# Later ones products for the norms, and one product with the values for both directions of a gated linear attention

## The reference

```
y = xf * lax.rsqrt(jnp.mean(xf * xf, axis=-1, keepdims=True) + EPS)
h = h + 0.5 * swiglu(rmsnorm(h, norm_gains[l, 0]), ...)
h = h + mixer(rmsnorm(h, norm_gains[l, 1]), ...)
h = h + 0.5 * swiglu(rmsnorm(h, norm_gains[l, 2]), ...)
```

```
att = jnp.where(mask, jnp.einsum('bhnid,bhnjd->bhnij', q_dec, k_inv), 0.0)
o_intra = jnp.einsum('bhnij,bhnjv->bhniv', att, vc)
...
o = (o_f + o_b)[:, :, pad:, :]
```

## Time and profile before

| | |
|---|---|
| median of 3 runs | 1885.31 us (1884.41 to 1885.64) |
| the profiled execution | 1884.92 us, of which the profile's span is 1883.6 us |
| granted TensorE clock, mean | 0.999 of full speed (2.4 GHz) |
| TensorE matmul busy | 1855.7 us, 99% of the span, 15211 instructions |
| VectorE busy | 1366.7 us, 73% |
| ScalarE busy | 1040.6 us, 55% |
| DMA | 365.92 MB, 194 GB/s in the mean |
| chain that ended last | TensorE 96%, ScalarE 2%, VectorE 1% |

### The profile page before, as it was taken

How to read it: one execution, slowest core, us unless ns; L and a number is a source line. 1 busy time by engine, 2 the same in 40 slices (tenths; PEclk the granted TensorE clock), 3 DMA queues, 4 the chain that set the end, 5 groups by cost and what they waited for, 6 DMA issues and landing times.

```text
span 1883.6 us, 36365 instructions
## 1 busy us (share of the span) xinstructions
PE 1855.7 (99%) x15211; PEld 1817.0 (96%) x15211; DVE 1366.7 (73%) x2353; ACT 1040.6 (55%) x1732; POOL 1.3 (0%) x8
## 2 busy tenths in 40 slices
PE   7999999999999999999999999999999999999998
PEld 7999998899999999999889999999999999999998
DVE  6777776576776678677658787698787558787744
ACT  6444564655444444456566455576565457656543
POOL 0000000000000000000000000000000000000000
PEclk9999999999999999999999999999999999999999
DMA  7776333356775577633235778454555554445553
GB/s 284 261 269 263 121 132 99 105 178 241 265 289 200 202 259 277 232 135 134 91 134 211 259 287 298 141 173 155 174 185 179 188 180 160 168 167 185 187 189 112
DMA packets 51811, 365.92 MB, mean 194 GB/s; under 512 B 6620, under 2 KB 8060, under 8 KB 9920
## 3 DMA queue, kind: packets, MB, share of 16 engines
q1 hardware_dynamic: 51648, 363.59, 55.2%
HBM read 362.52 MB, written 1.05 MB: 193 GB/s over the span
## 4 chain that ended last, share of the span: by engine, by line
PE 96%; ACT 2%; DVE 1%; issue 0%; DMA 0%; SPq 0%; DVEq 0%; ACTq 0%
PE bank L439 29%; PE bank L440 28%; PE bank L441 28%; PE bank L475 2%; PE bank L471 2%; PE bank L472 2%; PE bank L705 1%; PE bank L633 1%; PE bank L690 1%; PE bank L735 0%; PE bank L639 0%; PE bank L865 0%; PE bank L521 0%; ACT w_hi L1015 0%; PE bank L880 0%
## 5 line engine op out<-in xcount | busy, mean ns | idle before, releaser
L439 PE MATMUL bank<-xn_hi,w_hi 128*128 128x272 f32 (+3 forms) x2688 | 777.1, 289 | 1.7 <-DVE w_lo L1519 1.7
L441 PE MATMUL bank<-xn_lo,w_hi 128*128 128x272 f32 (+3 forms) x2688 | 764.3, 284 | 0.0
L440 PE MATMUL bank<-xn_hi,w_lo 128*128 128x272 f32 (+3 forms) x2688 | 764.2, 284 | 0.0
L439 PEld LDWEIGHTS bank<-xn_hi,w_hi 128*128 128x128 f32 (+1 forms) x2688 | 506.2, 188 | 9.4 <-issue 4.4
L440 PEld LDWEIGHTS bank<-xn_hi,w_lo 128*128 128x128 f32 (+1 forms) x2688 | 506.1, 188 | 1.2
L441 PEld LDWEIGHTS bank<-xn_lo,w_hi 128*128 128x128 f32 (+1 forms) x2688 | 506.8, 189 | 0.0
L1015 ACT ACTIVATE w_hi<-raw_a 128x1024 fp32r<-128x1024 f32 (+1 forms) x282 | 307.6, 1091 | 300.7 <-PE bank L441 263.9
L1015 ACT ACTIVATE w_hi<-raw_b 128x1024 fp32r<-128x1024 f32 (+1 forms) x282 | 307.5, 1091 | 282.3 <-PE bank L441 260.5
L1519 DVE TENSOR_TENSOR w_lo<-raw_a,w_hi 128x1024 fp32r<-128x1024 f32 (+1 forms) x282 | 356.5, 1265 | 135.5 <-ACT w_hi L1015 135.1
L1519 DVE TENSOR_TENSOR w_lo<-raw_b,w_hi 128x1024 fp32r<-128x1024 f32 (+1 forms) x282 | 356.6, 1265 | 133.0 <-ACT w_hi L1015 132.3
L439 PE MATMUL bank<-h_hi,w_hi 128*128 128x272 f32 (+1 forms) x704 | 201.7, 286 | 0.0
(11 more groups left out here) (316 smaller groups left out, 2624.2 us busy)
## 6 DMA issues: line engine op xcount, KB each, us to landing
raw_a<-in_weights SPq DMA_DIRECT2D x123, 1024.0 KB, 4.8
raw_b<-in_weights SPq DMA_DIRECT2D x123, 1024.0 KB, 4.8
ada_raw<-in_ada_w SPq DMA_DIRECT2D x48, 1024.0 KB, 5.0
raw_a<-in_weights SPq DMA_DIRECT2D x16, 1408.0 KB, 5.8
raw_b<-in_weights SPq DMA_DIRECT2D x16, 1408.0 KB, 5.9
c_rows<-in_c_rows SPq DMA_DIRECT2D x3, 512.0 KB, 5.8
raw_a<-in_weights SPq DMA_DIRECT2D x2, 768.0 KB, 4.1
raw_b<-in_weights SPq DMA_DIRECT2D x2, 768.0 KB, 4.2
```

The source lines that it names most:

```text
L439: pe.matmul(o, wh, xh, start=start, stop=False)
L440: pe.matmul(o, wl, xh, start=False, stop=False)
L441: return pe.matmul(o, wh, xl, start=False, stop=stop)
```

## The change

Two places are changed. First, `norm_sum` stands later within the leading steps: behind kk = 5 in the feed-forward stages of the first network (before: 1), behind kk = 3 in the first `ln1` stage (before: 2), behind kk = 2 in the mixers (before: 1). The stages `ff` and the second `ln1` keep kk = 2, and the very first stage keeps its place. Second, VectorE adds the two directions' masked scores of each head, and TensorE multiplies the sum with the values once instead of multiplying both. The sums lie in the first half of the tiles `full` and `gate` (`both_ways`); the second head pair waits for the last use of `full` by the first.

```
+def both_ways(c, j):
+    return (c.full, c.gate)[j][:, 0, :]
 ...
-            if stage != ("ffn", 0, 0) and kk == (2 if stage[0] in ("ln1", "ff") else 1):
+            if stage != ("ffn", 0, 0) and kk == (5 if stage[0] == "ffn" else 3 if stage == ("ln1", 0) else 2):
                 norm_sum(7, cols, stage)
 ...
-                    for d in range(2):
-                        pe.matmul(bank[b][:, c0:c0 + n], c.vtok[0:n, t, h * P:(h + 1) * P], c.att[2 * (b - 2) + d][0:n, c0:c0 + n], start=d == 0,
-                                  stop=False, skip_group_check=True)
+                    pe.matmul(bank[b][:, c0:c0 + n], c.vtok[0:n, t, h * P:(h + 1) * P], both_ways(c, b - 2)[0:n, c0:c0 + n], start=True,
+                              stop=False, skip_group_check=True)
 ...
-                    dve.copy_predicated(o[:, META:T], c.msk[:, d, META:T], bank[2 + j][:, d * SEQ:(d + 1) * SEQ]).then_inc(
-                        *k.up("gla_v", ("att", l, p) if d and j else None))
+                    dve.copy_predicated(o[:, META:T], c.msk[:, d, META:T], bank[2 + j][:, d * SEQ:(d + 1) * SEQ]).then_inc(*k.up("gla_v"))
+            if p:
+                dve.wait_ge(*k.at("x_lo", ("a", l, 1)))
+            dve.wait_ge(*k.newest("gla_v"))
+            for j in range(2):
+                dve.tensor_tensor(both_ways(c, j)[:, live], c.att[2 * j][:, live], c.att[2 * j + 1][:, live], ALU.add).then_inc(
+                    *k.up("gla_v", ("att", l, p) if j else None))
```

## The result

| | before | changed |
|---|---|---|
| median of 6 runs | 1885.47 us (1884.41 to 1886.71) | 1878.76 us (1877.55 to 1879.78) |
| ratio | | 0.9962, 95% interval 0.9952 to 0.9972 |
| profiled execution (span) | 1884.92 us (1883.6) | 1879.34 us (1878.0) |
| matmul records | 15211 | 15171 |

The kernel is 6.7 us faster by its median. The ratio is estimated from all runs and is not the quotient of the two medians, which is 0.9964; its interval is 5.3 to 9.1 us. Forecast were 1879.3 us and 6.0 us less.

The account below looks back on a forecast made before the run. TensorE's matmuls cover 99% of the span, so only removed matmuls and its gaps count. 3.57 us (products less additions) plus 2.41 us (ones products) save 5.98 us, giving 1879.3 us; range 1878.5 to 1880.1, with near rivals 1877.6 to 1881.2.

Parts of the forecast that it names:

- Products with the values: GLA head pairs of both layers: 40 fewer matmul records at 0.112 us each save 4.48 us.
- The additions: VectorE, after the masked copies: 0.88 us, hidden except layer 1's second head pair, which loses 0.86 us; its first loses 0.05.
- The ones products: Later placement in feed-forward, first `ln1` and mixer stages saves 2.41 us in sum.
- The three feed-forward terms: Removed waits for `sumsq`: 0.80 us in layer 1's first feed-forward, 0.37 in layer 0's second, 0.56 in layer 1's second.
- The `ln1` term: First `ln1` stage: one step of six matmuls moves into the wait, saving 0.72 us.
- The mixers: Both mixers: the 0.8 us wait moves to the second pair of units; nothing gained, 0.02 us lost in each.
- The cover of `rstd`: Feed-forward stages: later `rstd` delays unit 4's `w_lo`, but 2.6 us of room remain, so no price.
- Norms given back: Rival, 12%: feed-forward and `ln1` savings are lost to a wait further down; 1881.8 us, or 1880.5 if half is lost.
- gaining mixers: Rival, 7%: the mixers' new wait is short, so they gain after all; 1877.7 us.
- cheaper products: Rival, 4%: removed products are worth half, since the array sets the pace; 2.24 us less saved, 1881.5 us.
- Dearer additions: Rival, 10%: additions cost their upper bounds, 1.05 + 0.28 us; 1879.7 us, or 1880.5 if attention is delayed too.
- The slower rival: Rival, 2%: feed-forward's late `rstd` delays unit 4's split over 2.6 us, so TensorE waits for weights; 1888.3 us.

Follow-up runs that it names:

- `rec_only`: The changed kernel with all ones products back at their old places, so only additions and single product with the values: 1881.01 us, ratio 0.9977 to before.
- `adds_twice`: The changed kernel with both additions done twice, the second time behind a wait for the first: steps +0.16, 0.0, +0.67 and +5.45 us in the four head pairs.
- `ffn_at_2`: The changed kernel with the feed-forward stages' ones product behind kk = 2 in place of 5: 1877.91 us, one run.
- `mix_at_1`: The changed kernel with the two mixers' ones product back behind kk = 1: 1879.13 us, one run.
- `mix_at_3`: The changed kernel with the two mixers' ones product one step later, behind kk = 3: 1880.03 us, one run.
- `ffn_late`: The changed kernel with the ones product of all feed-forward stages behind the third unit: 1888.36 us, one run.
- `norm_only`: The kernel before with only the later ones products, without the additions: 1883.76 us, ratio 0.9989 to before.

## Why the prediction was right

**Products with the values.** Right in mechanism and size: 40 records at 0.112 us, -1.34 forecast and -1.34 measured twice. `rec_only` has the same steps. The table in the section "Back-to-back issue gap" of the Trainium skill ("TensorE: Matmul & The Clock Gate") would have given less than half, 2.0 us for all. The same section says that these are gaps of isolated matmuls, and gives about 81 ns for one of 128 columns in a stream with weight loads; by that, an estimate, the 32 large records are worth 2.6 us, where the trace's 0.112 gives 3.6. Neither figure holds for these fp32 products, and the trace decides.

**The additions.** Sized at 0.88 us, measured 0.87; hidden in layer 0 and in layer 1's first pair, a wait in its second as forecast. The loss there was put at 0.86 us and is about 0.76 (-0.90 gained, -0.14 left). The term that was too large is, for 0.10 of it, the time from the release to TensorE's start: I took 0.15 us from the ones product behind `sumsq`, and behind the additions it is 0.05 (927.97 to 928.02), so the wait is 0.64 in place of 0.77. The 0.09 us put down as lost behind a wait did show, as 0.11. `adds_twice` shows the room at the other places: 0.80 us more moved TensorE's start by 0.54 in layer 1's first pair (distance 0.66 in place of 0.12) and cost 0.11 behind it, so 0.26 us were free there, where I had put a loss of 0.05. In layer 0's first pair 0.65 were free, in its second at least 0.80.

**The ones products.** The three feed-forward terms are right within 0.01 us, and `ffn_at_2` shows that the part of the change that mattered was one step, not four. The `ln1` term was sized at 0.72 us and measured 0.82 against before. But `rec_only`, where this ones product wasn't moved, has a step of -0.09 at the same unit; against it the changed kernel steps by -0.73, the size forecast, and the passage with the two products itself went from 1.64 us to 0.93. The 0.09 isn't the move's.

**The mixers.** Zero, as forecast, and by the mechanism forecast: `mix_at_1` and `mix_at_3` show the second pair of units bound to the ones product, and with it to `rstd`. The loss of 0.02 us for each did not show.

**The cover of `rstd`.** Right: the split of unit 4 ended at 630.09 in layer 1's first feed-forward stage, which is the forecast 632.15 less the 2.06 us by which that profiled execution was ahead there. Its first use came at 632.80, so 2.7 us of room remained (forecast 2.6), and `ffn_late` used it up.

**What the sum missed.** Nothing of the change is missing: -5.98 against -6.25. The median moved by 6.7, which its interval allows. The forecast said nothing of TensorE's clock, and gave no reason. In the changed kernel's trace no stretch of half clock lies at a place that the change touches. But in the one run of `adds_twice` 0.8 us more of the same wait was followed by such a stretch and cost 5.4 us in all.

**The rivals.** Norms given back and gaining mixers are refuted by `norm_only` and the two mixer kernels, cheaper products by `rec_only`. Dearer additions were not found. The slower rival's mechanism exists, and starts where it was put, at 2.6 us more delay of the split (4.5 us in `ffn_late` left a wait of 1.9).

## What to carry to other kernels

Read a stage's start to its end before counting a removed wait: if the next thing on the engine hangs on the same signal, the wait moves and nothing is gained, and many small waits of 0.1 us hide it from any list. An operand that two products share is worth adding first when the adding engine has room behind its own release; the room must be read at every place apart, since TensorE came 1.6 us behind the copies at one and 0.26 at another. Where an engine waits for one reduced value, move it late enough to be ready and no later, and look for the same pattern in the places that the change leaves alone: the first stage had 1.9 us of it.

## What was not expected of the hardware

- Gaps of about 2 us on TensorE were followed by 3.4 us at 1.2 GHz in some executions and not in others: in the first stage in two traces of ten that have that gap, and in `ffn_late` at two of three gaps of 2.06, 2.06 and 2.19 us. A distance of 1.57 us, 5 us behind another of 0.78, was followed by 10 us at that level (`adds_twice`), and two of 0.77 by none. But a distance of 1.87 to 1.89 us with one of 0.62 some 4 us behind it, in layer 1's attention, was followed by none in any of the fourteen traces. The size of a gap alone doesn't tell.
- The program's first matmuls ran at the pace of 1.2 GHz for 3.2 to 5.7 us from one trace to the next, which moved the end of the first unit by up to 1.15 us.
- Fp32 matmul records of 16 and of 128 columns have the same distance, 0.112 us, in the products with the values.
- TensorE started 0.15 us after VectorE's release at the ones product and after 0.05 at the products with the values.
- The same products in another order (states ahead of values) cost 0.15 to 0.35 us more for each head pair.
